# Attention: one order of steps for all engines becomes a table for each engine

## What is computed

```python
def diff_attention(q, k, v, q_pos, k_pos, rel_bias, lam, subln_g, lam_init):
    s = jnp.einsum('bqhcd,bkhcd->bchqk', qf, kf) * (HEAD_DIM ** -0.5)
    s = jnp.where(mask, s + bias, -jnp.inf)
    p = jax.nn.softmax(s, axis=-1)
    w = p[:, 0] - lam * p[:, 1]
    o = jnp.einsum('bhqk,bkhe->bqhe', w, v.astype(jnp.float32))
    o = o * lax.rsqrt(jnp.mean(o * o, axis=-1, keepdims=True) + SUBLN_EPS)
    o = o * subln_g.astype(jnp.float32) * (1.0 - lam_init)
...
def stick_breaking_attention(q, k, v, q_pos, k_pos):
    z = jnp.einsum('bqhd,bkhd->bhqk', q.astype(jnp.float32), k.astype(jnp.float32)) * (HEAD_DIM ** -0.5)
    log_beta = jax.nn.log_sigmoid(z)
    log_rest = jnp.where(mask, jax.nn.log_sigmoid(-z), 0.0)
    suffix = lax.cumsum(log_rest, axis=3, reverse=True) - log_rest
    a = jnp.where(mask, jnp.exp(log_beta + suffix), 0.0)
    o = jnp.einsum('bhqk,bkhd->bqhd', a, v.astype(jnp.float32))
```

## Time and profile before

| what | value |
|---|---|
| median of 3 runs | 1515.75 us (1514.39 to 1516.41) |
| span of the profiled execution | 1514.8 us |
| first attention stage, 349.5 to 665.5 | 316.0 us |
| second attention stage, 665.5 to 963.0 | 297.5 us |
| mean granted clock of TensorE over the span | 0.944 |

### The profile page before, as it was taken

How to read it: one execution, slowest core, us unless ns; L and a number is a source line. 1 busy time by engine, 2 the same in 40 slices (tenths; PEclk the granted TensorE clock), 3 DMA queues, 4 the chain that set the end, 5 groups by cost and what they waited for, 6 DMA issues and landing times. The chain is left out here.

```text
span 1514.8 us, 26209 instructions
## 1 busy us (share of the span) xinstructions
PE 1325.4 (87%) x8895; PEld 960.1 (63%) x8895; DVE 797.1 (53%) x1118; ACT 665.4 (44%) x1086; POOL 144.9 (10%) x175
## 2 busy tenths in 40 slices
PE   7999999997898989778999898699749999999940
PEld 6878888885555656456656564588636666666720
DVE  4321122104555566547777778644466666666637
ACT  5410222013655565645656565422235556656612
POOL 1000000000000000100000000000012122222025
PEclk9999999998998999989999999899959999999975
DMA  6622332167686878547879794354377997632287
GB/s 204 205 88 74 127 125 86 70 228 240 224 278 207 302 249 305 177 161 232 277 257 325 244 323 154 119 167 153 135 273 277 405 413 271 216 117 89 84 289 258
DMA packets 159645, 319.15 MB, mean 211 GB/s; under 512 B 21815, under 2 KB 50906, under 8 KB 155418
## 3 DMA queue, kind: packets, MB, share of 16 engines
q1 hardware_dynamic: 146666, 274.48, 52.8%
q0 software_dynamic: 7200, 26.22, 5.1%
q10 hardware_dynamic: 5648, 16.78, 2.8%
HBM read 318.79 MB, written 55.77 MB: 247 GB/s over the span
## 5 line engine op out<-in xcount | busy, mean ns | idle before, releaser
L2400 DVE TENSOR_TENSOR w_gate_up_split<-w_gate_up,w_gate_up_split 128x2048 fp32r<-128x2048 f32 x64 | 143.8, 2289 | 109.4 <-ACT w_gate_up_split L2449 108.7
L2351 PE MATMUL gate_up_ps<-w_gate_up_split,slot_rows_T 128*128 128x512 f32 x768 | 186.0, 398 | 4.6 <-DVE slot_rows_T L2408 4.4
L327 PE MATMUL proj_ps<-w_in_split,x_T_hi 128*128 128x512 f32 x576 | 183.2, 394 | 0.0
L2351 PEld LDWEIGHTS gate_up_ps<-w_gate_up_split,slot_rows_T 128*128 128x128 f32 x768 | 143.3, 190 | 39.9 <-DVE slot_rows_T L2408 10.7
L1183 PE MATMUL turns_and_scores_ps<-ident,pages 128*128 128x128 f32 (+1 forms) x1088 | 149.2, 284 | 16.2 <-issue 5.7
L1183 PEld LDWEIGHTS turns_and_scores_ps<-ident,pages 128*128 128x128 f32 (+1 forms) x1088 | 124.3, 147 | 50.6 <-issue 49.9
L2449 ACT ACTIVATE w_gate_up_split<-w_gate_up 128x2048 fp32r x62 | 115.3, 1908 | 34.0 <-issue 34.0
L461 ACT ACTIVATE proj_rows<-proj_ps,sum_squares 128x512 f32<-128x512 f32 x36 | 24.8, 690 | 224.0 <-PE proj_ps L327 224.0
L327 PEld LDWEIGHTS proj_ps<-w_in_split,x_T_hi 128*128 128x128 f32 x576 | 108.7, 189 | 22.6
L2373 PE MATMUL expert_out_ps<-w_down,expert_act_T 128*128 x256 | 115.3, 593 | 1.3 <-ACT expert_out L2479 1.3
L1715 PE MATMUL mix_out_ps<-w_out_split,oT_split 128*128 128x512 f32 x432 | 105.1, 400 | 9.2 <-DVE oT_split L1777 9.2
(11 more groups left out here) (231 smaller groups left out, 1935.4 us busy)
## 6 DMA issues: line engine op xcount, KB each, us to landing
pages<-in_cache_s SPq DMA_DIRECT2D x256, 256.0 KB, 4.4
pages<-in_cache_d SPq DMA_DIRECT2D x226, 256.0 KB, 4.6
w_gate_up<-in_w_gate SPq DMA_DIRECT2D x34, 1024.0 KB, 8.6
w_gate_up<-in_w_up SPq DMA_DIRECT2D x34, 1024.0 KB, 10.5
w_down<-in_w_down SPq DMA_DIRECT2D x34, 1024.0 KB, 12.5
scratch_moe_out<-expert_out ACTq DMA_DIRECT2D x32, 512.0 KB, 4.0
w_in_now<-in_w_in SPq DMA_DIRECT2D x48, 256.0 KB, 2.9
pages_ahead<-in_cache_d SPq DMA_DIRECT2D x30, 256.0 KB, 3.5
```

Of the source, the lines that this page charges most:

```text
L327: last = pe.matmul(pj_ps[:, n % PJ_BANKS, :], h[:, k, at], w[g % 2][:, k, :], start=(k == 0 and m == 0), stop=(k == KC - 1 and m == 2))
L2351: last = pe.matmul(gu_ps[:, u, :], xT[:, u, a, k, :], gu_split[:, u, b, k, :], start=(k == 0 and m == 0), stop=(k == KC - 1 and m == 2))
L2400: dve.tensor_tensor(gu_split[:, u, 1, at, :].rearrange("p k (c n) -> p k c n", c=2), raw[:, at, :, :], gu_split[:, u, 0, at, :].bitcast(F3 ...
```

## The change

The planner goes, and with it its weights. In its place stands a table of letters, one per step, for each of the two stages and each of TensorE, VectorE and ScalarE. `steps_of` gives, for every kind of step, its steps in their natural order, and `engine_orders` takes the next one of a kind for each letter. SyncE walks TensorE's table. The rings of PSUM and page places follow TensorE's table too. The norm of a `DIFF` output gets a letter of its own (`n`), so on VectorE other steps can stand between the norm and the copy of the turned output. The two buffers of `k_pages_T` are now used by turns over the whole stage, not anew from the first in each turn. GpSimd's list, the instructions of each step and all sizes are as before.

```diff
-FIRST_KEYS, LAG, END_KEYS = 0.30, 0.02, 0.31
-WEIGH_AT, USE_AT, END_USE = 0.34, 0.42, 0.30
-SCORE_COST = {DIFF: 6, STICK: 12}
...
+STEPS = dict(s="score", m="soft", o="out", n="norm", t="turn_out", p="page", q="page_scores", k="peak", w="weigh",
+             h="share", u="turn", a="apply", r="rows", f="heads", z="store")
+ORDERS = {
+    DIFF: {
+        "PE": ("ppppsqssqpospppooqqsppppooqqsotopppppqqqtossspppsoqppussptooaaaqqtppppoouaaaaaqqsstoopptootpssaqaaoo"
...
+def steps_of(kind):
...
+def engine_orders(kind):
+
+    out = {}
+    for engine, letters in ORDERS[kind].items():
+        left = {name: iter(steps) for name, steps in steps_of(kind).items()}
+        out[engine] = [(STEPS[c], *next(left[STEPS[c]])) for c in letters]
     return out
...
-    uses = [step for step in attention_plan(kind) if step[0] in ("page", "apply")]
+    uses = [step for step in engine_orders(kind)["PE"] if step[0] in ("page", "apply")]
...
-        plan = attention_plan(kind)
+        orders = engine_orders(kind)
+        plan = orders["PE"]
...
-                                             kT_page[:, g % 2, KIND_BLOCKS * e + b, 0:n],
+                                             kT_page[:, (it * S_GROUPS + g) % 2, KIND_BLOCKS * e + b, 0:n],
...
-                def turn_out(it, i):
+                def norm(it, i):
                     dve.wait_ge(sub_rstd.sem, sub_rstd.after(it, i))
                     dve.wait_ge(oT_done.sem, oT_done.after(it, i - 1))
                     dve.tensor_scalar_mul(o_norm[:, :], o_rows[:, i % 2, :], stat[:, i % 4, 7:8])\
                        .then_inc(o_normed.sem, 1)
+
+                def turn_out(it, i):
                     dve.wait_ge(oT_done.sem, oT_done.after(it, i))
...
-                for name, *args in plan:
+                for name, *args in orders["DVE"]:
                     if name in steps:
                         steps[name](*args)
...
-                for name, *args in plan:
+                for name, *args in orders["ACT"]:
                     if name in steps:
                         steps[name](*args)
```

127 lines of the change are left out of this document (47 added, 80 removed).

## The result

| | before | after |
|---|---|---|
| median of the runs | 1515.66 us (1514.39 to 1516.41) | 1413.92 us (1413.38 to 1415.06) |
| span of the profiled execution | 1514.8 us | 1412.5 us |
| first attention stage: length, TensorE idle | 313.7, 45.8 us | 235.6, 3.8 us |
| between the stages, no matmul | 2.6 us | 25.0 us |
| second attention stage: length, TensorE idle | 295.2, 25.5 us | 247.8, 2.0 us |

The ratio is 0.9335, 95% interval 0.9321 to 0.9350: 102 us less, where the forecast was 30 less and the range ended at 1456. The stages are measured here from their first matmul to the end of their last one; "lower clock level" adds up the time in which the granted clock was 0.50 (1.2 GHz).

A forecast was written before the change was run, and what follows sets the result against it. TensorE, busy 87% of the span, was taken as the bound, with 76 us idle in the two attention stages. First stage -34, second -17, edge +21.5: together -29.5 from 1514.8, giving 1485 us, range 1456 to 1518.

The forecast's parts named there:

- The case in which nearly all of it goes: Rival, both stages: nearly all remaining idle time goes, with the clock's 8 us and few new waits; 1446 us, chance 0.10.
- The other idle time: Both attention stages: TensorE waits besides the turning's shrink as makers stand further ahead of users; -5 and -10 us.
- The clock: First attention stage: less idle time raises the mean granted clock from 0.93; -4 us, nothing in the second.
- The new waits on the PSUM ring: Both stages: runs of pages wait for copies out of three PSUM places; +8 and +4 us, near the low end.
- Turning of the prompt output: First stage: more TensorE work before the normed output's turn removes most of its 24.6 us wait; -22 us.
- the ring: Three PSUM places, named as what is late next after the turning; as rival, TensorE waits there, 1522 us, chance 0.14.
- Steps of one kind: Both stages: 114 and 113 fewer changes of kind on TensorE, at 0.10 to 0.20 us each; -11 us each.
- a change of kind costs nothing: Rival, both stages: the gap read is only a modelled matmul's tail, so joining steps saves nothing; 1507 us, chance 0.12.
- The seam: Between the attention stages: the earlier last store holds SyncE's next-stage page loads back while TensorE stands; +21.5 us.

The follow-up runs named there:

- e11: Changed kernel with TensorE waiting for eight GpSimd memsets (2.04 us) at 32 places of the second stage; 1445.9 us.
- e12: Changed kernel with TensorE waiting for sixteen GpSimd memsets (4.13 us) at 32 places of the second stage; 1557.8 us.
- e10: e2 with each prompt output product two places further up in all three tables, nearer to the turned weights it uses; 1479.4 us.
- e6: Changed kernel with VectorE taking the shared steps in TensorE's order, ScalarE keeping its own table; 1429.0 us.
- e2: Changed kernel with VectorE and ScalarE both taking the shared steps in TensorE's new order; 1434.6 us.
- e9: Changed kernel with TensorE waiting for three GpSimd memsets (0.73 us) at 32 places of the second stage; 1414.0 us.
- e3: Kernel before with only the turn of a tile's output, norm still tied to it, moved after the next tile's product; 1529.5 us.
- e5: Changed kernel with runs of applied pages in TensorE's table broken up by other steps, 27 and 41 more changes of kind; 1433.9 us.
- e4: Kernel before with only the first stage's last store moved beside the one ahead of it; 1537.9 us.
- e1: Changed kernel with the first stage's last store moved back to the end of TensorE's table, which SyncE walks; 1401.2 us.
- e7: Kernel before, one list for all engines, with its planner gathering like steps into runs on a time grid; 1550.5 us.

## Why the prediction was wrong

The direction was right, and so were the mechanisms of the turning, of the kinds and of the seam, the last within a microsecond. The size was missed because three terms that together stood at -7 us (other idle time -15, clock -4, new waits +12) measured at -65 (-41.5, -23.5, 0). Another 14 us came from the changes of kind (-36 instead of -22).

**The other idle time** (-5 and -10) is the step that failed most, by 26.5 us. It was taken apart into one chain that the change moves, counted in full, and a rest, of which a quarter and a third were let go, as a guess beside median leads. Measured: TensorE's idle time fell from 71.3 us to 5.8 in the two stages, 65.5 us, where 22 + 5 + 10 = 37 were forecast; less the turning's 24.0 the rest fell by 41.5, not 15. The case in which nearly all of it goes had chance 0.10 and came in, and more. It was refused because leads hardly moved in the second stage (3.8 to 4.1 us). But the lead that was looked at, from turned weights to their product, was not the one at which TensorE waited. Its wait in before's first stage was one of 0.6 us, and in the second there was none that ends with the copied weights; the larger ones there stood before other steps:

```profile
PE o_ps L1161 <- ACT weights_T L1502: 0.6, 1, 0.6
```

```profile
PE turns_and_scores_ps L1216 <- ACT betas L1478: 4.6, 3, 2.6
PE turns_and_scores_ps L1200 <- DVE k_pages_T L1350: 2.7, 3, 1.4
```

The second stage's idle time went from 25.5 to 2.0 us while this lead stayed, so it says nothing of what the other leads do. By e11 and e12 TensorE's queue also forgives some 1.2 us of lateness where it is full, and the list of waits shows only the excess. That the new order has hardly any idle time because nothing in it is late by more than that fits its waits (none over 0.9 us behind the stage's start), but isn't shown. e10 shows that this lead does bring waits once it is cut from 4.2 to 2.4 us. Also, the 4.9 us at the start of the first stage were taken out of the 48.1 by mistake: they lie ahead of 349.5. And 2.2 us of the 48.1 are the seam itself, so the rest was 21.2 us and not 18.6.

**The clock** (-4 and 0). The first stage's mean was read as 0.93 and taken to 0.96, the second's left alone. Both came out at 0.99. Time at the lower level fell by 37.3 and 12.3 us, TensorE's busy time in it by 34.2 and 12.8; a half of that is 17.1 and 6.4 us. The term hangs on the one before, which the sum didn't say: before, 15 and 10 idle pieces of the two stages were longer than 1 us, 31.4 and 18.0 us together, and after none was. e12 shows the clock going down with such pieces, e11 that it stays up with pieces of about 0.9 us. Where idle time of that kind goes, the clock's half comes on top.

**The new waits on the PSUM ring** (+8 and +4). They are not there: 3.8 and 2.0 us are all the idle time that is left, of whatever kind, and none of it is a wait for a page's copy. The reason given for the low end (VectorE and ScalarE have orders of their own) is worth some 15 and 6 us by e6 and e2, as idle time and clock. By e9 and e11 there is a second one, which wasn't known: a copy that is late by less than some 1.2 us isn't felt where the queue is full.

**Turning of the prompt output** (-22). Its wait fell from 24.6 to 0.6 us. Right in place and size, but the later turn alone doesn't bring it: in e3, on the old list and with the norm still tied to the turn, 17.1 us of the wait stay and one for the copied weights comes up. "What is late next" was asked, and answered with the ring; in e3 it is the copied weights. What the norm's own place has of the gain is open.

**Steps of one kind** (-11 in each stage). Busy time fell by 36.0 and 23.7 us; less the clock's 17.1 and 6.4, there remain 18.9 us for 114 and 17.3 us for 113 changes: 0.17 and 0.15 us each, between the 0.10 and 0.20 read from starts in the earlier trace rows, while the low end was taken. It is a remainder, put down to the changes because e5, whose edit only adds such changes, comes to 0.11 to 0.16. One group of TensorE, before and then after:

```profile
L1231 PE MATMUL sample_o_ps<-pages,sample_weights_T 128*32 128x256 f32 x512 | 41.0, 399 | 0.0
```

```profile
L1197 PE MATMUL sample_o_ps<-pages,sample_weights_T 128*32 128x256 f32 x512 | 31.6, 381 | 0.0
```

The mean of one fell by 4.5%, the group's busy time by 23%: in runs the applied pages overlap each other's ends. Such a row also counts time that overlaps with neighbours of another kind, so it shows where runs help and not how much the stage gains. The rival "a change of kind costs nothing" had the chance 0.12 and falls with e5.

**The seam** (+21.5) measured +22.4, and e4 gives +21.7 for it by itself. The load rate was inside its bounds: 20.12 us for 32 loads, 0.63 each, between 0.57 and 0.75. DMA's share was 0.94 to 1.05 meanwhile, so whether SyncE or the full DMA engines set that rate isn't separated. What the prediction missed is what stood behind it: with the store last the seam is still 7.2 us (e1), because the new order frees the last places late.

With what was measured the sum is: first stage -42.0 idle, -17.1 clock, -18.9 kinds; second -23.5, -6.4 and -17.3; seam +22.4; elsewhere +0.8. That is -102.0, against -102.3 between the spans. It closes because the kinds are what is left of the busy time.

Open is what of the idle time's fall is owed to which lead. Only e10 moves mainly one lead, and that is one at which the kernel before hardly waited; e5, e6, e2 and e10 show only that four different disturbances of the new order each bring 10 to 41 us of it back, and e3 and e7 that a later turn and longer runs, each alone on the old list, bring none of it.

## What to carry to other kernels

When an order is rebuilt as a whole, don't let idle time go by shares of a guess: ask whether any wait must remain (an engine near full, a chain with no work to put beside it). Here VectorE and ScalarE had 12% or more of their time to spare after the gain, and nearly all idle time went. Before a lead is used to refuse a gain, look whether TensorE waits at that lead at all. Price idle pieces of TensorE by length, with the lower clock behind the long ones. Don't judge an order by a single move: two of its features, tried alone, brought more waits. And whatever is moved in one queue, read what the same table does to the others: one letter of SyncE's cost 22 us, and giving it back with a split of the loads gave the fastest kernel, 1393.3 us.

## What the runs showed of the hardware

- TensorE's queue stood a median of 1.10 us (0.78 to 2.03) ahead of the array at 32 places of a stage that was busy 99%. There waits of 0.73 us cost nothing; of 2.04 us each 0.87 showed, of 4.13 us 2.83.
- Idle pieces of about 0.9 us left the clock up: granted clock 1.00 over the 265 us in which nearly all of e11's 30 us of idle time lie. Pieces of about 3 us (e12) brought 115 us more at 1.2 GHz for 90 us of idle time, and the kernel lost 1.6 us for each us idle.
- A change from one kind of step to another on TensorE cost 0.11 to 0.16 us of busy time at full clock in e5; the remainder between the two kernels comes to 0.15 to 0.17.
- 32 loads of 256 KB in a row from one queue took SyncE 20.12 and 20.40 us, 0.63 and 0.64 each, while in the first case the DMA engines moved 291 to 390 GB/s.
